# A modulation matrix multiplied without splitting it, on four column strips, and its tiles put elsewhere

## The reference

```python
for i in range(2):                       # first block
    h = rmsnorm(x, mix_norm[i]);  z = h @ w_in[i]
    y_a = rglru_branch(...) @ w_br_a[i]  # convolution, gates, linear recurrence (LRU)
    y_b = mla_branch(...) @ w_br_b[i]    # 8 heads, low-rank q and kv, rotary
    y_c = fox_branch(...) @ w_br_c[i]    # 8 heads, a cumulated forget gate as decay
    x = x + (g[0]*y_a + g[1]*y_b + g[2]*y_c) @ w_o[i]
    hf = rmsnorm(x, ffn_norm[i]) @ w_gate_up[i]
    x = x + (silu(hf[:, :D_FF]) * hf[:, D_FF:]) @ w_down[i]
    x = x + sigmoid(rmsnorm(x, ple_norm[i]) @ w_ple_gate[i]) * (p[i] @ w_ple[i])
x = rmsnorm(x, final_norm)
# second block: x and a context of 256 tokens
for i in range(2):
    sh1, sc1, g1, sh2, sc2, g2 = split(silu(c) @ ada_w[i] + ada_b[i])   # the modulation, [1024, 6144]
    # the same with c_ctx for the context
    a = rms_norm(h, norm_g[i, 0]) * (1 + sc1) + sh1
    h = h + g1 * (pool_mix(a) if i == 0 else attn_mix(a_ctx, a))
    m = rms_norm(h, norm_g[i, 1]) * (1 + sc2) + sh2
    h = h + g2 * (relu(m @ mlp_w1[i]) ** 2 @ mlp_w2[i])
out = rms_norm(h, final_g)
```

## Time and profile before

| | us |
|---|---|
| median of 3 runs | 2063.09 (2056.41 to 2064.56) |
| the profiled execution, its own time | 2063.15 |
| its span | 2061.4 |
| TensorE busy | 1858.9 (90%) |
| GpSimd busy | 1317.3 (64%) |
| ScalarE busy | 960.9 (47%) |
| VectorE busy | 880.7 (43%) |

### The profile page before, as it was taken

How to read it: one execution, slowest core, us unless ns; L and a number is a source line. 1 busy time by engine, 2 the same in 40 slices (tenths; PEclk the granted TensorE clock), 3 DMA queues, 4 the chain that set the end, 5 groups by cost and what they waited for, 6 DMA issues and landing times.

```text
span 2061.4 us, 36518 instructions
## 1 busy us (share of the span) xinstructions
PE 1858.9 (90%) x12966; PEld 1717.9 (83%) x12966; DVE 880.7 (43%) x1959; ACT 960.9 (47%) x1403; POOL 1317.3 (64%) x451
## 2 busy tenths in 40 slices
PE   5997998999979889999999955799999988889997
PEld 5886898999969877999999944688888866778997
DVE  3677444323335685453223377321121256443223
ACT  5634556544665435556445653533232343355443
POOL 6664588988886744698988952544444433136885
PEclk9999999999989898999999966899999989898999
DMA  6443355665554532465656651423232222124553
GB/s 218 154 154 103 116 187 189 209 201 195 199 194 144 177 116 90 154 210 195 208 189 201 205 177 48 141 93 102 90 102 95 97 79 88 39 70 138 185 185 110
DMA packets 67873, 301.31 MB, mean 146 GB/s; under 512 B 7424, under 2 KB 9728, under 8 KB 67584
## 3 DMA queue, kind: packets, MB, share of 16 engines
q1 hardware_dynamic: 66240, 296.69, 43.2%
q10 hardware_dynamic: 1472, 2.43, 0.3%
HBM read 298.04 MB, written 1.05 MB: 145 GB/s over the span
## 4 chain that ended last, share of the span: by engine, by line
issue 33%; PE 32%; POOL 31%; DVE 2%; ACT 1%; DVEq 1%; POOLq 1%; ACTq 0%
POOL wlo L729 31%; PE bank L763 10%; PE bank L766 10%; PE bank L767 10%; PE bank L1071 0%; DVE bank L1992 0%; PE bank L1074 0%; PE bank L1075 0%; PE bank L1110 0%; POOLq L733 0%; PE bank L1098 0%; DVE split_acts L1523 0%; DVEq L2151 0%; ACT bank L1395 0%; ACTq L1404 0%
## 5 line engine op out<-in xcount | busy, mean ns | idle before, releaser
L729 POOL TENSOR_TENSOR wlo<-raw,whi 128x1280 fp32r<-128x1280 f32 x447 | 1317.1, 2964 | 724.5 <-ACT whi L1144 722.8
L763 PE MATMUL bank<-split_acts,whi 128*128 128x256 f32 (+1 forms) x3556 | 1099.0, 309 | 75.8 <-DVE split_acts L1523 49.0
L766 PE MATMUL bank<-split_acts,whi 128*128 128x256 f32 (+1 forms) x3556 | 1084.3, 305 | 0.0
L767 PE MATMUL bank<-split_acts,wlo 128*128 128x256 f32 (+1 forms) x3556 | 1082.9, 305 | 0.0
L763 PEld LDWEIGHTS bank<-split_acts,whi 128*128 128x128 f32 x3556 | 696.7, 196 | 122.1 <-issue 60.3
L1144 ACT ACTIVATE whi<-raw 128x1280 fp32r<-128x1280 f32 x447 | 562.8, 1268 | 412.0 <-PE bank L763 349.1
L766 PEld LDWEIGHTS bank<-split_acts,whi 128*128 128x128 f32 x3556 | 697.8, 196 | 22.6 <-issue 0.2
L767 PEld LDWEIGHTS bank<-split_acts,wlo 128*128 128x128 f32 x3556 | 697.1, 196 | 23.2
L775 PE MATMUL bank<-whi,split_acts 128*128 128x256 f32 x384 | 112.3, 322 | 42.1 <-POOL wlo L729 39.5
L2024 DVE SCALAR_TENSOR_TENSOR acts<-bank,acts 128x256 f32<-128x256 f32 x120 | 54.1, 480 | 222.4 <-PE bank L767 222.4
L2038 DVE TENSOR_SCALAR acts<-bank 128x512 f32<-128x512 f32 (+1 forms) x64 | 35.7, 558 | 203.2 <-PE bank L767 203.2
(11 more groups left out here) (234 smaller groups left out, 1535.4 us busy)
## 6 DMA issues: line engine op xcount, KB each, us to landing
raw<-in_stream SPq DMA_DIRECT2D x448, 640.0 KB, 3.8
acts<-in_x SPq DMA_DIRECT2D x1, 1024.0 KB, 6.4
acts<-in_ctx ACTq DMA_DIRECT2D x1, 1024.0 KB, 7.4
out<-acts SPq DMA_DIRECT2D x8, 128.0 KB, 2.0
acts<-in_const ACTq DMA_DIRECT2D x1, 832.0 KB, 10.0
acts<-in_const SPq DMA_DIRECT2D x1, 772.0 KB, 9.0
acts<-in_p ACTq DMA_DIRECT2D x2, 256.0 KB, 5.4
acts<-in_par SPq DMA_DIRECT2D x1, 86.0 KB, 2.0
```

The source lines that it names most:

```text
L729: nc.gpsimd.tensor_tensor(wlo[slot][:, :], raw[slot][:, :], whi[slot][:, :].bitcast(F32), ALU.subtract).then_inc(lo_ready, 1)
L763: first = nc.tensor.matmul(out_ap, w_hi, hi_act(k), start=(k == 0), stop=False)
L766: nc.tensor.matmul(out_ap, w_hi, lo_act(k), start=False, stop=False)
L767: last = nc.tensor.matmul(out_ap, w_lo, hi_act(k), start=False, stop=(k == k_tiles - 1))
```

## The change

1. **An ada tile** is 8 four-byte matmuls, without splitting: the raw float32 chunk is read straight from its slot (`modulation`). 128 x 32 of `silu_c` is stationary, 256 columns stream; the four row blocks of a chunk go to partitions 0, 32, 64 and 96 of the bank, so the four partial sums stay apart. A tile has two chunks of 8 atoms. A `pe.drain()` stands behind it. VectorE copies 128 x 256, and the turn adds the four strips by a product over 128 rows.
2. **The ring** has two kinds of chunks in a planned order (`chunk_plan`): split ones as before, and modulation ones, whose slot is free when TensorE has read it (`ada_used`). 468 chunks, of which 372 are split (447 before). `keep_ahead` looks at positions in the raw ring. A layer has 124 split and 12 modulation chunks, block 2 124 and 72.
3. **Places.** Each layer keeps only 6 ada tiles, all in the head. Block 2 has 36: two each before `ss first`, `ss 0 0`, `pool 0`, `ss 0 1`, `w1 0 0 0` and `w1 0 0 4`, one before each further fourth `w1` or `w2` of its first MLP and two more at its end, and 8 in the second layer's projections up to `v 0`. The gains of the norms (`norm_gains`) are computed one at a time, where needed.
4. **Attention.** `pair_lo` and ScalarE's rounding of a pair stand a step later, the LRU's last parts are taken at steps 2 to 4 and not 1 and 2, the series of log1p is done in two halves in steps 4 and 5, and the rest of the decay in step 6. The values wait for one pair's output more.
5. **Start.** No split before the mix norm and one inside it (after k = 5); the activations of the modulation are set up in fewer operations. `ones` has 128 columns.

The diff, cut to its core (`attended`, `pair_out` and the rest of the attention's order as it is in the last three pieces):

```diff
@@ -104,11 +109,7 @@
 HEAD_TILES, _n = with_modulation(HEAD_TILES, {("ss", "mix"): 2, ("ss", "q"): 1, ("ss", "kv"): 1, ("qn", 0): 1,
-                                              ("rotq", 0): 1}, 0, end=("rotq", 1))
-MID_TILES, _n = with_modulation(MID_TILES, {("g", 2, j): 1 for j in (0, 2, 4, 6)}, _n, _n)
-TAIL_TILES, _n = with_modulation(TAIL_TILES, {("ss", "ffn"): 2, ("hg", 0, 3): 1, ("hg", 0, 7): 1,
-                                              ("hg", 1, 3): 1, ("hg", 1, 7): 1, ("ss", "ple"): 2}, _n,
-                                 end=("pg", 4))
+                                              ("rotq", 0): 1}, 0, flush=(("rotq", 1),))
 assert _n == LAYER_ADA
...
@@ -146,11 +147,34 @@
 ATOM_SPAN, LAYER_ATOMS = first_atoms()
-LAYER_CHUNKS = -(-LAYER_ATOMS // (CHUNK_ATOMS * RING)) * RING
-def last_chunk(span):
-    return max(span[1] - 1, 0) // CHUNK_ATOMS
+SPLIT_CHUNKS = -(-LAYER_ATOMS // (CHUNK_ATOMS * RING)) * RING
+ADA_CHUNKS = 2
+ADA_ATOMS = 2 * KT // ADA_CHUNKS
+def chunk_plan(tiles, spans, split_chunks):
+    order, at, splits, adas, late = [], {}, 0, 0, []
+    for t in tiles:
+        if t[0] == "ada":
+            run = [("ada", adas + i) for i in range(ADA_CHUNKS)]
+            adas += ADA_CHUNKS
+            if splits:
+                late += run
+            else:
+                order += run
+        while splits * CHUNK_ATOMS < spans.get(t, (0, 0))[1]:
+            order += [("split", splits)] + late
+            splits, late = splits + 1, []
+        at[t] = len(order) - 1
+    return order + late + [("split", n) for n in range(splits, split_chunks)], at
+ORDER, RAW_AT = chunk_plan(TILES, ATOM_SPAN, SPLIT_CHUNKS)
+RAW_OF = {c: i for i, c in enumerate(ORDER)}
+LAYER_CHUNKS = len(ORDER)
+LAYER_ADA_CHUNKS = LAYER_CHUNKS - SPLIT_CHUNKS
+assert LAYER_CHUNKS % RING == 0
...
@@ -186,9 +208,13 @@
     + [("ss", 1, 1)] + mlp_tiles(1) + [("ss", "last")])
-TILES2, _n = with_modulation(TILES2, {("ss", "first"): 2, ("ss", 0, 0): 2, ("pool", 0): 2,
-                                      ("ss", 0, 1): 6}, DEPTH * LAYER_ADA, DEPTH * LAYER_ADA,
-                             ("w1", 0, 0, 0))
+TILES2, _n = with_modulation(
+    TILES2,
+    {("ss", "first"): 2, ("ss", 0, 0): 2, ("pool", 0): 2, ("ss", 0, 1): 2, ("w1", 0, 0, 0): 2, ("w1", 0, 0, 4): 2,
+     **{(w, 0, q, j): 1 for q in range(QUARTERS) for w in ("w1", "w2") for j in (0, 4) if (w, q) != ("w1", 0)},
+     ("w2", 0, 3, 2): 1, ("w2", 0, 3, 6): 1, ("ss", 1, 0): 1, ("q", 0): 2, ("q", 4): 1, ("k", 0): 2, ("k", 2): 1,
+     ("v", 0): 1},
+    DEPTH * LAYER_ADA, flush=(("ss", 0, 1), ("w2", 0, 0, 0), ("v", 0)))
 assert _n == ADA_TILES
...
@@ -708,12 +743,24 @@
                 fetch(slot, slot)
-            with sp.Fori(1, N_CHUNKS // RING) as r:
-                for slot in range(RING):
-                    sp.wait_ge(lo_ready, r * RING + (slot - RING + 1))
-                    sp.dma_start(raw[slot][:, :], stream[bass.ds(r * RING + slot, 1)].rearrange("a p n -> (a p) n"))\
-                        .then_inc(raw_in[slot], 16)
+            def raw_free(order, c, splits_before, adas_before):
+                kind, n = order[c]
+                if kind == "split":
+                    sp.wait_ge(lo_ready, splits_before + (n + 1))
+                else:
+                    sp.wait_ge(ada_used, adas_before + (n + 1))
+            with sp.Fori(0, DEPTH) as lay:
+                for c in range(LAYER_CHUNKS):
+                    raw_free(ORDER, c, lay * SPLIT_CHUNKS, lay * LAYER_ADA_CHUNKS)
+                    sp.dma_start(raw[c % RING][:, :],
+                                 stream[bass.ds(lay * LAYER_CHUNKS + (c + RING), 1)].rearrange("a p n -> (a p) n"))\
+                        .then_inc(raw_in[c % RING], 16)
+            for c in range(len(ORDER2) - RING):
+                raw_free(ORDER2, c, FIRST_SPLIT2, FIRST_ADA2)
+                fetch(c % RING, FIRST_CHUNK2 + c + RING)
             for t in range(KT):
...
@@ -767,20 +815,23 @@
-            def modulation(b, lay, base):
-                for k in range(KT):
-                    w_hi, w_lo, opens = weights(lay, base, 2)
-                    s4 = silu_c[:, k * P:(k + 1) * P]
-                    first = nc.tensor.matmul(b[:, 0:256], s4, w_hi, start=(k == 0), stop=False)
-                    if opens:
-                        first.then_inc(slots_used, 1)
-                    last = nc.tensor.matmul(b[:, 0:256], s4, w_lo, start=False, stop=(k == KT - 1))
+            def modulation(b, order, chunks_before):
+                for part in range(ADA_CHUNKS):
+                    c = order[("ada", Cursor.ada)]
+                    Cursor.ada += 1
+                    pe.wait_ge(raw_in[c % RING], chunks_before * (16 // RING) + (c // RING + 1) * 16)
+                    for strip in range(4):
+                        k = part * 4 + strip
+                        last = nc.tensor.matmul(b[32 * strip:32 * strip + 32, 0:256], silu_c[:, 2 * k:2 * k + 32],
+                                                raw[c % RING][:, strip * 256:(strip + 1) * 256],
+                                                start=(part == 0), stop=(part == ADA_CHUNKS - 1))
+                    last.then_inc(ada_used, 1)
                 return last
                 for i in range(4):
-                    last = nc.tensor.matmul(b[:, 2 * i:2 * i + 2], rows[0:4, i * P:(i + 1) * P], C("pair")[0:4, :],
+                    last = nc.tensor.matmul(b[:, 2 * i:2 * i + 2], rows[:, i * P:(i + 1) * P], C("pair"),
                                             start=True, stop=True)
...
@@ -825,7 +876,8 @@
                     if kind == "ada":
-                        modulation(b, lay, base).then_inc(gemm_done, 1)
+                        modulation(b, RAW_OF, lay * LAYER_CHUNKS)
+                        pe.drain().then_inc(gemm_done, 1)
                         return
...
@@ -1135,18 +1188,11 @@
-            def split(lay, base, chunk):
-                g = base(lay, chunk)
-                act.wait_ge(slots_used, g + 1)
-                act.wait_ge(raw_in[chunk % RING], (base(lay, chunk - chunk % RING) // RING) * 16 + 16
-                            if isinstance(g, int) else lay * (LAYER_CHUNKS // RING * 16) + (chunk // RING + 1) * 16)
-                sc.activation(whi[chunk % RING][:, :], raw[chunk % RING][:, :], ACT.Copy).then_inc(hi_ready, 1)
-            def ahead(lay, base, chunk):
-                while Split.chunk <= chunk + AHEAD:
-                    split(lay, base, Split.chunk)
-                    Split.chunk += 1
+            def split(n, source, splits_before, chunks_before):
+                act.wait_ge(slots_used, splits_before + (n + 1))
+                act.wait_ge(raw_in[source % RING], chunks_before * (16 // RING) + (source // RING + 1) * 16)
+                sc.activation(whi[n % RING][:, :], raw[source % RING][:, :], ACT.Copy).then_inc(hi_ready, 1)
...
@@ -1181,8 +1222,8 @@
                         sc.activation(tile(hi, k), tile(x, k), ACT.Copy, scale=Cp(g, k)).then_inc(nhi_ready, 1)
-                        if name == "mix" and k in (2, 5):
-                            keep_ahead(("ada", k // 3))
+                        if name == "mix" and k == 5:
+                            keep_ahead(("ada", 0))
...
@@ -1311,8 +1349,10 @@
                                 decay_mask(i // 2 + 1)
-                            if kind == "mla" and i in (1, 2):
-                                part = i + 1
+                            if i >= 3 and i % 2:
+                                attended(kind, i // 2 - 1 + (0 if kind == "mla" else 4))
+                            if kind == "mla" and i in (2, 3):
+                                part = i
                                 act.wait_ge(lru_done, lay * 4 + part + 1)
...
@@ -1321,8 +1361,8 @@
                                 of_tile(t)
-                        if i and i % 2 == 0:
-                            attended(kind, i // 2 - 1 + (0 if kind == "mla" else 4))
+                        if i == 8:
+                            attended(kind, 3 + (0 if kind == "mla" else 4))
...
@@ -1884,23 +1923,31 @@
                             lru_core(i + 2)
-                        if kind == "mla" and i in (1, 2):
-                            lru_lo_part(i + 1)
+                        if i in (3, 5, 7):
+                            pair_lo(kind, first_pair + i // 2 - 1)
+                        if kind == "mla" and i in (3, 4):
+                            lru_lo_part(i - 1)
                         if i < 8:
+                        if i and i % 2 == 0:
+                            pair_out(kind, first_pair + i // 2 - 1)
+                            if i == 8:
+                                pair_lo(kind, first_pair + 3)
                         if kind == "mla" and i == 3:
                         if kind == "mla" and i == 4:
-                            half_log1p_series(f_s, f_s2, f_p)
+                            half_log1p_start(f_s2, f_p)
                         if kind == "mla" and i == 5:
```

(4 more changed lines are left out.)

177 lines of the change are left out of this document (92 added, 85 removed).

## The result

The changed kernel takes 2045.62 us (median of 4 runs, 2043.8 to 2049.38), the kernel before 2063.41 in the same comparison: ratio 0.9923, interval 0.9897 to 0.995. It is faster, clear of noise, by 16 us (0.8%) by the ratio and 17.8 by the medians: inside the range, but less than half of the 39 forecast. Its profiled span is 2044.9 us, 16.5 less than before.

A forecast was written before the change was run, and what follows sets the result against it. TensorE was taken to bound the dense stretches, VectorE or a chain the others. Layers and heads -56.4 us and block 2 +17 gave -39.4, from 2063.15 to 2024 us; 80% range 1998 to 2050.

The forecast's parts named there:

- The tile's price: One modulation tile on four column strips, with what follows it, was to cost 1.35 us; bounds 0.96 and 3.9.
- fv's starvation: In fv, TensorE was to wait 7.3 us for split 13's low part, split only behind the LRU activations; +8.8 with slow starts.
- the gates, feed-forward, PLE: Per layer, fewer tiles and turns: gates -9.9 us, feed-forward -10.0, PLE norm -1.3 and its late turn -1.2.
- the first MLP: Block 2's first MLP, with no idle time, was to take in 18 tiles and 9 to 10 turns: +34 us.
- The +5.7 from kr to the scores: Per layer, fv's wait and slow starts (+8.8 us) less what four modulation tiles and their waits give back; bounds -3.1 and +9.
- Attention (-3 per layer): With pair_lo a step later, ScalarE's one long wait in MLA was to go: -3 us per layer, bounds 0 and -6.
- u to kr (0): The stretch from u to kr in each layer was forecast to change by 0 us.
- wo (-2.85, measured -8.2): Ahead of the feed-forward norm, its sum was to come 3.55 us earlier without tiles, less 0.7 for a slow start: -2.85 per layer.
- Block 2's head (-20, measured -13.9): Before ss01, two tiles stand instead of six and the ten low parts in a row go: -20 us.
- Behind the MLP (+6, measured +14.8): Of the last 8 tiles, behind block 2's first MLP, four waits for VectorE were to hide most: +6 us.
- the one in which fv does not starve: Rival, 15%: ScalarE reaches split 13 early or fv starts late enough, 2 x 8.8 us goes: 2006 us.
- the ring as a brake of the MLP: Rival, 8%: modulation chunks hold two of four raw slots, splits land late in the MLP, 36 us in all: 2060 us.

The follow-up runs named there:

- e7_old_places: The changed kernel, with its product, ring and attention, but the modulation tiles in the places of the kernel before: 2064.27 us, ratio 1.0005.

## Why the prediction was wrong in size, and where it held

**Held.** The tile's price (1.35 forecast, 1.3 measured); fv's starvation with its place, cause and size; the gates, feed-forward, PLE, and the first MLP within 1 us each. The +5.7 from kr to the scores is right as a mean (+3.8 and +7.0); that the two layers lie on both sides of it is the clock. The change of width between full-size products costs no more than the values' row had shown, and strips without a row group of their own do overlap: 2 x 0.43 and not eight times. Of the pages weighed, the Trainium skill (TensorEngine Tiling (Array Packing), Key Properties) has a drain at a change of mode; here going to the strips costs about 0.1 us, and coming back lies in the 0.3 us that a tile at full width has too. The Trainium skill (TensorE: Matmul & The Clock Gate, Part 3) gives three column strips a speedup of 2.38; here four have 3.4 (3.62 to 1.07).

**Where the 22.9 us went.** Against the sum: attention 10.2, u to kr 9.4, behind the MLP 8.8, block 2's head 6.1. For it, by luck: wo 10.7. Without this last gain the kernel would be faster by 6 us and not by 16.

**Attention (-3 per layer) and u to kr (0): the step that failed.** The working looked at how many splits go, "in dense stretches they are hidden, so I book nothing", and not at when GpSimd makes the low parts that are left, and beside what. Ahead of the changed places ScalarE has fewer splits in hand, since the look-ahead counts modulation chunks too (13 before the LRU's activations; 22 in the kernel before, the modulation's own among them), so the low parts come later and in bursts: four from 134.0 us on, after 18.17 us of idle time, on the LRU's second half, in which VectorE has two SBUF inputs; six up to 52.7 on the convolution. VectorE then waits for a whole instruction at a time, as the three sizes show (0.4 without, 1.7 beside a half, 3.0 beside a whole low part).

In attention this made the first two steps 5.4 and 5.9 us longer, and the kernels in which the low parts were moved bring them back (17.1 and 17.2 against 16.3). The rest of attention did get shorter, by 3.8 and 3.3 us, much as the -3 said, but the new order gave little of it: with the old one the rest is as short to 0.1 us in layer 0 and 1.6 longer in layer 1. ScalarE's wait that the forecast named went (10.4 us in layer 0's MLA before, 1.7 in the changed kernel, 9.7 with the old order), and one of 6.7 came in step 7, where the exponentials now stand behind the decay. In u to kr, putting one low part behind the convolution took 2.0 and 2.9 of the +4.3 and +5.1, so about half of that row is shown.

The Trainium skill (SBUF — State Buffer, Who interferes with whom) states just this: the two engines share one port pair, held exclusively for a whole instruction. The runs agree with it. The forecast saw VectorE busy 62.22 of MLA's 76.30 us and did not ask what ran beside it.

**wo (-2.85, measured -8.2).** Two parts. The norm's own is 3.7 us shorter, and it stays 3.4 shorter in `e7_old_places`, with its two tiles still there: at 1.33 us they hide in the wait. (The row at 356.45 in the earlier trace rows is a turn's bias, L1560; the norm's last sum, L1611, ended at 356.5, which leaves the sum as it was.) The other 4.5 are in wo 0 and wo 1 and were not forecast. TensorE's wait for VectorE's split there, in the kernel before and in the changed one:

```profile
PE bank L763 <- DVE split_acts L1524: 3.5, 2, 2.4
```

```profile
PE bank L811 <- DVE split_acts L1562: 0.7, 1, 0.7
```

With it go wo 0's and wo 1's slow starts (6.9 and 4.3 us before, 3.9 and 2.9 after). In `e7_old_places` both are as before the change (3.2 us of waits, 6.7 and 4.3 us), so this part comes with the four tiles that left the gates. That it is the collision again, in the other direction, is argued: what VectorE's records last too long, counted as above, falls from 12.7 to 7.4 us between the gates and the norm.

**Block 2's head (-20, measured -13.9).** The part ahead of ss 0 1 came (28.6 us to 10.3, -18.3). The stretch from ss first to ss 0 0 is 3.1 us longer and the one from ss 0 1 to w1 1.0. The landing of 10.0 us was taken as given. It is a row of a time in which the queue was kept back by low parts; modulation chunks free their slots when read, and eight refills ran beside the constants.

**Behind the MLP (+6, measured +14.8).** "Four such waits hide most" failed. A wait for VectorE ahead of q 0 does not hide a turn that itself waits for VectorE's copy, and between the waits the projections are dense.

Of the rivals, the one in which fv does not starve fell, and the ring as a brake of the MLP (36 us) did not show: TensorE is busy 373.63 of 377.30 us there. Open are the other half of u to kr, and the old product in the new places.

## What to carry to other kernels

When work leaves an engine, ask when the rest of it now runs, and beside what: GpSimd's busy time fell by 220 us, and what VectorE lost beside it hardly at all (85 us to 80). A look-ahead that counts positions of a shared ring shrinks as soon as something else takes positions in it; count the work that one engine makes for the next. And where filler goes into a wait, it must not need the engine that is waited for.

## What the runs showed of the hardware

A VectorE operation on 128x256 float32 with two SBUF tensors as inputs takes 0.42 to 0.48 us, and up to 3.2 beside GpSimd's 2.96 us instruction, 1.6 to 1.8 beside half of one. TENSOR_SCALAR from SBUF to SBUF waits too (0.35 us, up to 2.8). RECIPROCAL with one SBUF input takes 1.75 us in both cases, and an operation that reads a bank and SBUF 0.42. In the profile such a wait looks like work: the record is longer, and no idle time stands before it. Four column strips with 128 rows each take 1.07 us for eight four-byte products of 256 columns, 3.62 at full width; going from full width to the strips costs about 0.1 us.
